# Moving the residual's row stores and input loads from SyncE's queue to ScalarE's at the hand-over to the FFN

## The reference

```
h = rmsnorm(x, g_mix);  z = h @ w_in;  a, b, v = split(z)
u = a * sigmoid(b);  u = causal depthwise conv(u), 31 taps;  u = silu(layernorm(u))
q = multi-scale trailing means of v, minus v, per-group matmul, scale
x = x + concat(u, q) @ w_out                  # x1, the residual after the mixer
h = rmsnorm(x, g_ffn);  gu = h @ w_gate_up
x = x + (silu(gu[:F]) * gu[F:]) @ w_down
gate = sigmoid(rmsnorm(x, g_ple_gate) @ w_ple_gate);  e = rmsnorm(p @ w_ple_up, g_ple_post)
out = rmsnorm(x + gate * e, g_final)
```

## Time and profile before

| | us |
|---|---|
| median of 3 runs | 993.18 (992.72 to 995.23) |
| the profiled execution, its time | 994.86 |
| the profiled execution, its span | 992.9 |
| TensorE busy in it | 980.3 |
| VectorE busy in it | 710.7 |
| ScalarE busy in it | 458.1 |

### The profile page before, as it was taken

How to read it: one execution, slowest core, us unless ns; L and a number is a source line. 1 busy time by engine, 2 the same in 40 slices (tenths; PEclk the granted TensorE clock), 3 DMA queues, 4 the chain that set the end, 5 groups by cost and what they waited for, 6 DMA issues and landing times.

```text
span 992.9 us, 12311 instructions
## 1 busy us (share of the span) xinstructions
PE 980.3 (99%) x4447; PEld 812.3 (82%) x4447; DVE 710.7 (72%) x982; ACT 458.1 (46%) x704; POOL 380.4 (38%) x288
## 2 busy tenths in 40 slices
PE   9999999999999999999999999999999999999996
PEld 7888888888788888888888888888888888888885
DVE  6899999996798355354454544553677888887897
ACT  7625347404363333423333333333444665676865
POOL 3445889710245544444354353442000000012555
PEclk9999999999999999999999999999999999999999
DMA  7620112558724234233332432412999788657432
GB/s 257 140 87 40 45 41 116 202 172 190 211 64 153 60 109 121 89 107 95 117 107 80 133 107 64 148 64 99 355 370 322 233 304 268 198 159 201 152 107 106
DMA packets 154799, 148.74 MB, mean 150 GB/s; under 512 B 56507, under 2 KB 110291, under 8 KB 154739
## 3 DMA queue, kind: packets, MB, share of 16 engines
q1 hardware_dynamic: 153536, 147.56, 46.7%
q10 hardware_dynamic: 1202, 0.40, 0.2%
HBM read 109.92 MB, written 38.01 MB: 149 GB/s over the span
## 4 chain that ended last, share of the span: by engine, by line
PE 70%; DVE 2%; DMA 2%; SPq 1%; issue 1%; POOL 1%; ACT 1%; POOLq 0%; DVEq 0%; ACTq 0%
PE ps L1659 23%; PE ps L1661 23%; PE ps L1660 23%; SPq L627 1%; DMA xn_scratch<-scr 1%; DMA scr<-xn_scratch 1%; PE ps L1708 0%; DVE resid L2181 0%; DVE scr L2063 0%; DVE ftmp L2522 0%; POOL rs L785 0%; DVE resid L2525 0%; DVE act_lo L2035 0%; SPq L632 0%; ACT junk L1056 0%
## 5 line engine op out<-in xcount | busy, mean ns | idle before, releaser
L782 POOL TENSOR_SCALAR ss<-ss 128x1 f32<-128x1 f32 x38 | 14.5, 381 | 322.0 <-ACT junk L1056 286.6
L2129 DVE SCALAR_TENSOR_TENSOR ps<-resid,convw,ps 128x512 f32<-128x512 f32 x190 | 127.4, 749 | 0.0
L1659 PE MATMUL ps<-ring_hi,ring_lo 128*128 128x512 f32 x308 | 119.9, 389 | 0.1
L1661 PE MATMUL ps<-ring_hi 128*128 128x512 f32 x308 | 119.8, 389 | 0.0
L1660 PE MATMUL ps<-ring_lo,ring_hi 128*128 128x512 f32 x308 | 119.8, 389 | 0.0
L1659 PE MATMUL ps<-act_hi,bs_lo 128*128 128x512 f32 x240 | 93.5, 389 | 0.0
L1660 PE MATMUL ps<-act_lo,bs_hi 128*128 128x512 f32 x240 | 93.4, 389 | 0.0
L1661 PE MATMUL ps<-act_hi,bs_hi 128*128 128x512 f32 x240 | 93.4, 389 | 0.0
L2288 DVE TENSOR_TENSOR gtmp<-ps,gtmp 128x512 f32<-128x512 f32 x22 | 15.2, 691 | 95.6 <-PE ps L1661 95.6
L1042 ACT ACTIVATE ring_hi<-raw 128x512 fp32r<-128x512 f32 x89 | 51.9, 625 | 60.5 <-PE ps L1661 58.1
L2035 DVE TENSOR_TENSOR ring_lo<-raw,ring_hi 128x512 fp32r<-128x512 f32 x89 | 58.0, 688 | 22.9 <-ACT ring_hi L1042 22.8
(11 more groups left out here) (281 smaller groups left out, 2620.7 us busy)
## 6 DMA issues: line engine op xcount, KB each, us to landing
raw<-in_w_gate_up SPq DMA_DIRECT2D x44, 512.0 KB, 5.2
raw<-in_scratch SPq DMA_DIRECT2D x52, 256.0 KB, 3.3
raw<-in_w_down SPq DMA_DIRECT2D x52, 256.0 KB, 4.2
in_scratch<-in_s SPq DMA_DIRECT2D x44, 256.0 KB, 3.4
in_scratch<-gtmp SPq DMA_DIRECT2D x33, 256.0 KB, 2.3
keep<-in_w_down SPq DMA_DIRECT2D x32, 256.0 KB, 4.1
keep<-in_scratch SPq DMA_DIRECT2D x25, 256.0 KB, 3.6
resid<-in_x SPq DMA_DIRECT2D x8, 512.0 KB, 6.9
```

What stands on the lines that cost most here:

```text
L782: pool.tensor_scalar(ss[:, n:n + 1], ss[:, n:n + 1], 1.0 / D, EPS, ALU.mult, ALU.add)\
L1659: pe.matmul(dst, w_lo_, m_hi, start=start, stop=False, skip_group_check=onto)
L1661: return pe.matmul(dst, w_hi_, m_hi, start=False, stop=stop, skip_group_check=onto)
L2129: dve.scalar_tensor_tensor(out=conv_c if k == last_odd else acc, in0=u_all[:, c, k + h * BANK:k + (h + 1) * BANK], scalar=convw[:, c * 32 ...
```

## The change

The stores of x1 for tiles 0 to 5, and the loads of the x tiles 2 to 7 that follow them, are taken from SyncE. ScalarE issues them instead, one store and one load directly behind the square of the tile. SyncE keeps the stores of tiles 6 and 7, in the place where they were. The number and size of the transfers are the same, and so are the semaphores that they raise. The waits on `rows_added` that stood ahead of the six stores on SyncE's queue go too: on ScalarE the wait ahead of the square serves both.

```diff
-            def store_x1(t):
-                sp.wait_ge(rows_added, 2 * (t + 1))
-                sp.dma_start(x1_dram[t], xres[:, t % 4, :]).then_inc(x1_stored[t % 4], DMA)
-                if t + 2 < TT:
-                    load_x(t + 2, raw_b[:, t % 2, :])
-
-            store_x1(0)
-            store_x1(1)
             store_xn(0)
             store_xn(1)
             load_xn(0)
             load_xn(1)
             store_xn(2)
-            store_x1(2)
-            store_x1(3)
             load_xn(2)
             store_xn(3)
             load_xn(3)
-            store_x1(4)
             store_xn(4)
             load_xn(4)
-            store_x1(5)
             sp.wait_ge(fs4_ok, 2)
             sp.wait_ge(fa_lo, 6)
             sp.wait_ge(fa_hi, 6)
             load_quad(1)
-            store_x1(6)
-            store_x1(7)
+            for t in range(TT - 2, TT):
+                sp.wait_ge(rows_added, 2 * (t + 1))
+                sp.dma_start(x1_dram[t], xres[:, t % 4, :]).then_inc(x1_stored[t % 4], DMA)
...
             def square_after(t, norm, count):
                 act.wait_ge(rows_added, count)
                 square(t, norm)
+                if t < TT - 2:
+                    act.dma_start(x1_dram[t], xres[:, t % 4, :]).then_inc(x1_stored[t % 4], DMA)
+                    act.dma_start(raw_b[:, t % 2, :], x_v[t + 2]).then_inc(x_in[t + 2], DMA)
```

## The result

The changed kernel is slower, and the prediction had its sign wrong:

| | median us (range, runs) | against before (95% interval) | span and mean granted clock of the profiled execution |
|---|---|---|---|
| before | 993.18 (992.46 to 995.23, 7) | | 992.9, 0.998 |
| changed | 996.45 (996.26 to 998.97, 7) | 1.0037 (1.0028 to 1.0047) | 994.4, 0.998 |

What follows compares the result with a forecast made beforehand. The prediction took TensorE to bound the kernel, with 1.63 us of stalls to win in the hand-over and all other terms zero: 993.18 - 1.63 = 991.5 us, range 990.5 to 994.0.

Steps and rivals of the forecast that it cites:

- The bound, and what can pass to the end: TensorE bounds the kernel; the change acts only at 205 to 290 us, and its effect there reaches the end undiminished.
- The sum against the median: Whole kernel: 1.63 us taken off the 993.18 us median of the runs before, giving 991.5 us.
- The three stalls: TensorE waits ahead of rows_out(6), turn(5, 1) and turn(6, 1), losing 0.30, 0.21 and 1.12 us, all expected to go.
- Point 1: SyncE around load_xn(2): twelve issues leave, its pieces take 3.38 instead of 7.20 us, block_turn(2) starts up to 3.7 us earlier.
- Point 2: Hand-over on TensorE: earlier VectorE work removes waits of 0.30, 0.21 and 1.12 us, the last with 0.48 us to spare.
- rival A: Ahead of turn(6, 1): the third wait stays in part or whole, 0.51 us won, 992.7 us; chance 0.20.
- Point 3: ScalarE around its squares: twelve added issues at 0.45 us each, covered by slack, cost nothing on the path.
- Rival C: ScalarE is held by its four issues of tiles 2 and 3: 5.8 us slower, 999.0; chance 0.07 beyond 0.3%.
- Point 5: ScalarE's stores beside SyncE's queue: load_xn(0) can only gain, load_xn(1) can lose within 3.6 us of cover; term zero.

## Why the prediction was wrong

**The bound, and what can pass to the end:** right. The whole effect lies between 205 and 290 us, and TensorE has no gap from there to 500 us. From its first product behind turn(7, 1) (at 281.42 and 279.36 us in the two traces of before, 282.97 and 282.25 in those of the changed kernel) to the end of the span it is 711.4 to 711.6 us in all four.

**The sum against the median: wrong.** The three stalls (1.63 us) were real in the profiled execution of before, and I took them off the median of the runs as if the median execution had them. The prediction notes that the profiled execution was 1.68 us above the median, and doesn't draw the conclusion: 1.68 is about the 1.63 that I meant to win. The second trace, at 990.9 us, has none of the three. Against that execution this term is 0 and not -1.63.

**Point 1, relief of SyncE:** half right. load_xn(2)'s pieces are issued in 2.74 us (I said 3.4), but they start 3.6 us later than before instead of at the same time: I counted what the transfers leave behind at their old place, and not what they do to load_xn(1) and store_xn(2) at the new one. block_turn(2) starts at 247.40 (I said 241.8), and not for want of the data: it has no wait for a DMA, since VectorE itself is late behind block_turn(1).

**Point 2, the three stalls:** the first two went in the changed kernel too, though not for the reason given: add_x(4) ends at 251.83, 1.9 us later than before, and normed(5) at 260.82, 0.4 us earlier and not 4, while TensorE itself came over 2 us later. The third stayed at 0.84 us in the trace, by the mechanism of rival A: block_turn(4) waits 1.93 us for load_xn(4) (0.78 before), and the chain from the end of add_x(6) to the end of normed(6), kept at 7.84 us in the sum with 0.48 us to spare, takes 8.98 us (264.01 to 272.99).

**Point 3, ScalarE:** right, and too careful. The twelve issues take 0.33 to 0.49 us beside the square, the lower bound. Rival C, the only one on the slower side, had the right sign and the right four transfers with the wrong victim: not ScalarE's queue but SyncE's load.

**Point 5, contention: this is the step that failed.** It says that load_xn(1) can lose, that block_turn(1) has 3.6 us of cover, and puts the term at zero without ever sizing the delay. It measures 5.1 to 5.9 us, and 1.8 to 2.7 us of it reach TensorE. ScalarE also issued the transfers with the start of the squares and not behind their end: at 224.36 and 227.03, where the store of tile 2 and that of tile 3 had stood at 232.03 and 233.34, so 6 to 8 us earlier and not 4 to 6. The help that point 5 saw for load_xn(0) didn't come either: it is issued from 220.91 us, and from 220.85 in the second trace of before. The trace of before would have given the size: 4 x 512 KB at the 372 GB/s that the engines move there from 216.0 to 221.5 us are 5.6 us. load_xn(4), the second place, wasn't looked at, although the trace of before has a wait of 0.78 us for its landing ahead of block_turn(4). It costs 0.001 in the time.

**The size:** the changed kernel's first trace loses 2.48 + 0.84 = 3.32 us at these places, and that of before 1.63: 1.7 us between them, where the spans differ by 1.5 (992.9 to 994.4). Against an execution of before without stalls it is the whole 3.3 us, and the medians differ by 3.27. Where the clock drops as well, 1.6 us come on top, in the one trace that has it.

## What to carry to other kernels

The order on one queue is worth something. Here large transfers that stood behind a latency-critical one on the same queue didn't slow it, even when brought forward, and on another engine's queue they did, by about their bytes over the engines' rate. Before moving an issue, list what is in flight at its new time, work out that delay, and set it against the cover of each reader and of what is queued behind the reader. A profiled execution that is slower than the median may owe that to the very stalls one means to remove; take a second trace before taking them off the median.

## What the runs showed of the hardware

- A DMA issue on ScalarE started with the square ahead of it in program order (both at 224.36) and took 0.33 us beside it. I had expected it to push the next instruction back.
- Small rows (128 bytes each) on one queue landed 2.8 us later with 1 MB of large rows beside them on the other, and 5.1 to 5.9 us later with 2 MB. The large ones' issues took 0.33 to 0.49 us in the changed kernel; one of 0.81 us is in the run that puts them beside load_xn(2).
- After 2.54 us without work, TensorE's granted clock went from 1.00 to 0.50 about 1.5 us after it had started again, and stayed there for about 3.4 us. In the two traces of the changed kernel, with gaps of 2.32 and 1.64 us at the same place, it stayed at 1.00.
